# A gated-linear-attention stage written in a new order, on one core of a Trainium2 chip

## What is computed

```python
q, k, v, r, glr = jnp.split(proj, ODD_SPLITS, axis=-1)
gate_logit = glr @ w_gate2.astype(jnp.float32) + b_gate.astype(jnp.float32)
log_a = (jax.nn.log_sigmoid(gate_logit) / GLA_TAU).reshape(B, T, GLA_HEADS, GLA_DK)
# per chunk, with b the running sum of log_a in the chunk
w = jnp.exp(jnp.where(causal[None, :, :, None, None], diff, -jnp.inf))
scores = jnp.einsum('bihd,bjhd,bijhd->bhij', qc, kc, w)
o = (jnp.einsum('bhij,bjhe->bihe', scores, vc)
     + jnp.einsum('bihd,bhde->bihe', qc * jnp.exp(b), s))
s = (s * jnp.exp(b_last)[..., None]
     + jnp.einsum('bjhd,bjhe->bhde', kc * jnp.exp(b_last[:, None] - b), vc))
# then
o = head_rms(o) * norm_w.astype(jnp.float32)
mix = (jax.nn.silu(r) * o.reshape(B, T, GLA_VALUE)).astype(h.dtype) @ w_out
```

## Time and profile before

| | |
|---|---|
| median of 3 runs | 2778.07 us (2776.79 to 2779.69) |
| profiled execution, its own time | 2778.14 us |
| its span | 2776.3 us |
| PE busy | 2638.2 us (95%) |
| DVE, ACT, POOL busy | 1361.3, 643.9, 853.0 us |
| mean granted clock of PE | 0.959 |

### The profile page before, as it was taken

The page is one execution under the profiler, slowest core; times in us unless marked ns, Lnnn a source line. Parts: engine busy times, 40 slices in busy tenths (PEclk is TensorE's granted clock), DMA queues, the critical chain, the costliest instruction groups (busy, mean ns, idle before and its releaser), DMA issues.

```text
span 2776.3 us, 38625 instructions
## 1 busy us (share of the span) xinstructions
PE 2638.2 (95%) x15232; PEld 2516.0 (91%) x15232; DVE 1361.3 (49%) x2146; ACT 643.9 (23%) x1111; POOL 853.0 (31%) x383
## 2 busy tenths in 40 slices
PE   7999879999999999999989999897999999999998
PEld 7898639999999999999878888787999999999997
DVE  6763355553344344436565656554553443343345
ACT  3610142321011011113223434432230110011013
POOL 3332103333333333333211112112433333333340
PEclk9999959999999999999989989888999999999999
DMA  3011002111111111112101010102111111111111
GB/s 133 31 56 39 31 25 103 46 46 46 47 39 46 47 46 46 39 45 110 39 18 54 25 54 25 54 18 110 43 42 46 46 46 39 47 46 46 46 54 65
DMA packets 39152, 137.63 MB, mean 50 GB/s; under 512 B 5952, under 2 KB 9664, under 8 KB 37712
## 3 DMA queue, kind: packets, MB, share of 16 engines
q1 hardware_dynamic: 32192, 104.55, 11.4%
q10 hardware_dynamic: 6800, 30.71, 2.9%
HBM read 120.36 MB, written 14.88 MB: 49 GB/s over the span
## 4 chain that ended last, share of the span: by engine, by line
issue 54%; PE 30%; POOL 14%; DVE 1%; DMA 1%; POOLq 1%; ACT 0%; SPq 0%; ACTq 0%; DVEq 0%
PE PS L498 30%; POOL WH L468 8%; POOL WL L471 6%; DMA WR<-ws 0%; DVE RA L1250 0%; DVE X L1299 0%; DMA X<-xT 0%; POOLq L467 0%; POOLq L479 0%; DVE X L1260 0%; POOLq L470 0%; PE PS L623 0%; SPq L441 0%; DVE X L1311 0%; PE PS L549 0%
## 5 line engine op out<-in xcount | busy, mean ns | idle before, releaser
L498 PE MATMUL PS<-RA,WH 128*128 128x384 f32 (+1 forms) x4608 | 1134.3, 330 | 36.0 <-issue 13.0
L498 PE MATMUL PS<-RB,WH 128*128 128x384 f32 (+1 forms) x4272 | 1060.0, 332 | 4.1 <-DVE X L1260 4.1
L468 POOL TENSOR_TENSOR WH<-WR,ZERO 128x1024 fp32r<-128x1024 f32 x185 | 355.4, 1921 | 1843.0 <-PE PS L498 1833.9
L498 PEld LDWEIGHTS PS<-RA,WH 128*128 128x128 f32 x4608 | 818.3, 189 | 47.8 <-issue 31.4
L498 PEld LDWEIGHTS PS<-RB,WH 128*128 128x128 f32 x4272 | 761.3, 190 | 19.6 <-issue 11.9
L498 PE MATMUL PS<-RA,WL 128*128 128x384 f32 (+1 forms) x2304 | 755.8, 328 | 0.0
L498 PE MATMUL PS<-RB,WL 128*128 128x384 f32 (+1 forms) x2136 | 701.4, 328 | 0.0
L471 POOL TENSOR_TENSOR WL<-WR,WH 128x1024 fp32r<-128x1024 f32 x185 | 480.3, 2596 | 14.5
L498 PEld LDWEIGHTS PS<-RA,WL 128*128 128x128 f32 x2304 | 435.3, 189 | 0.0
L1260 DVE TENSOR_TENSOR X<-PS,X 128x384 f32<-128x384 f32 x360 | 189.7, 534 | 440.7 <-PE PS L498 440.7
L498 PEld LDWEIGHTS PS<-RB,WL 128*128 128x128 f32 x2136 | 405.2, 190 | 0.0
(11 more groups left out here) (195 smaller groups left out, 1739.1 us busy)
## 6 DMA issues: line engine op xcount, KB each, us to landing
WR<-ws SPq DMA_DIRECT2D x189, 512.0 KB, 3.3
X<-xT ACTq DMA_DIRECT2D x8, 544.0 KB, 7.8
EB<-xT ACTq DMA_DIRECT2D x8, 544.0 KB, 8.1
x_spill<-X ACTq DMA_DIRECT2D x1, 4352.0 KB, 12.1
EB<-x_spill ACTq DMA_DIRECT2D x8, 544.0 KB, 7.1
GA<-st_gla ACTq DMA_DIRECT2D x4, 1024.0 KB, 5.3
glas_o<-GA ACTq DMA_DIRECT2D x4, 1024.0 KB, 3.9
yT<-X SPq DMA_DIRECT2D x16, 192.0 KB, 1.9
```

What stands on the lines that cost most here:

```text
L468: nc.gpsimd.tensor_tensor(WH[:, slot, :], WR[:, slot, :], ZERO[:, 0:1].to_broadcast([P, 1024]), ALU.add).then_inc(w_high, 1)
L498: return nc.tensor.matmul(out, lhsT, rhs, start=start, stop=stop, skip_group_check=True)
```

## The change

The stage's list is written anew, and with it the emitted parts:

- **All gate logits first.** The weight tile of "low" holds its 16 columns three times (at 0, 32, 64), and so does the gate weight. Item GL rounds both stacks on ACT and makes the remainder of one copy of each on DVE (L1620), so that one matmul over 96 partitions (L770) gives the three products of the split. The 12 logit matmuls (L, banks 6 and 7 in turn) stand in the projections of k0 and v0; softplus and sums (SPA, SPD) are done per head over all 1088 tokens, into tiles of X.
- **Chunks pipelined.** C1 and C2 become A and B. At place k of 36 the list has A of chunk k+1, S, B of chunk k, S; transposed keys and values and scores have two tiles each (gKVT, gSC). The state products move from A to B. Preparation of the next group (KD, DE, X, XE, Q, P) stands in the first two of each three places; the levels are scored from 6 down to 0, and level 0 takes the keys as they are, which saves a difference, an exponential and a product.
- **Samples third from last.** Chunk 8 stands between chunks 5 and 6; its eight updates are four pairs (CB), with one masked-key product for all eight (L1739).
- **GNM** has one matmul, since DVE adds the two squares first (L1769).
- **Roundings ahead.** MIX rounds and splits six of the eight tiles of the output projection's input before the list ends, and two after it.

The diff's core:

```diff
+ORDER = [0, 1, 2, 3, 4, 5, 8, 6, 7]
+    x = lambda v: [("X", e, v), ("XE", e, v)]
+    q = lambda v: [("Q", e, v)]
+    return [[[("KD", e), ("DE", e)] + x(6) + x(5), x(4) + q(6), x(3) + q(5) + x(2)],
+            [q(4) + x(1) + [("XE", e, 0)], [("P", e)] + q(3) + q(2), q(1) + q(0)]]
...
+    s = low + q0 + [("GL",), ("L", 0, 0)] + k0[:1] + [("L", 0, 1), ("SPA", 0, 0, 1)] + k0[1:2] + [("L", 0, 2)] + k0[2:]
+    s += [("SPD", 0, 0, 1), ("SPA", 0, 1, 3)] + L(1) + v0[:1] + [("SPD", 0, 1, 3)] + L(2) + v0[1:2] + L(3)
+    first, then = prepare(0)
+    s += [("SPA", h, 0, 3) for h in range(1, GH)]
+    s += first[0] + first[1] + v0[2:] + first[2] + v1[:1] + then[0] + then[1] + v1[1:2] + then[2]
+    s += [("SPD", 1, 0, 3)] + v1[2:] + [("A", 0, 0), ("SPD", 2, 0, 3), ("SPD", 3, 0, 3)]
     for h in range(GH):
...
+            if k + 1 < len(PLACES):
+                s.append(("A",) + PLACES[k + 1])
+            if p % 3 == 0 and e:
                 s.append(("GNM",) + divmod(e - 1, 3))
+            s += prep[0] + mine[:1]
+            if last:
+                s += [("MIX", 0), ("MIX", 1)]
+            s.append(("B", h, c))
+            if p % 3 == 0 and e:
+                s.append(("GN2",) + divmod(e - 1, 3))
+            if c == LAST:
+                s += [("CB", h, 0)] + mine[1:] + [("CB", h, 1)] + prep[1] + [("CB", h, 2), ("CB", h, 3)] + prep[2]
             else:
+                s += prep[1]
+                if last:
+                    s += [("MIX", 2), ("MIX", 3)]
+                s += mine[1:] + prep[2]
+            if p % 3 == 2:
+                s.append(("GN1", h, p // 3))
+    s += [("MIX", 4), ("GNM", GH - 1, 2), ("MIX", 5), ("GN2", GH - 1, 2), ("GMIX",), ("MIX", 6), ("MIX", 7)]
...
+                    pe.wait_ge(gl_ready, 2)
+                    if i < 2:
+                        pe.wait_ge(rs_log, 3 * 3)
+                    else:
+                        pe.wait_ge(lg_read, i - 1)
+                    nc.tensor.matmul(PS[:, 6 + i % 2, 0:size], WGH[:, GDK * h:GDK * (h + 1)], GLH[:, s:s + size],
                                      start=True, stop=True).then_inc(lg_done, 1)
...
+                elif kind == "GL":
+                    dve.wait_ge(gl_high, 2)
+                    for out, of in ((WGH[64:96, :], WG2[64:96, :]), (GLH[32:64, :], GLR[32:64, :])):
+                        V.tensor_tensor(out, of, out.bitcast(F32), ALU.subtract).then_inc(gl_ready, 1)
...
+                elif kind == "MIX":
+                    k = item[1]
+                    if k == 3:
+
+                        dve.wait_ge(gsb_stored, 16 * GH)
+                    if k == 6:
+                        dve.wait_ge(go_done, len(PLACES))
+                        dve.wait_ge(gp_stored, 16 * GH)
+                    low(4, k, RA1, None)
```

More of the change, by code:

```diff
@@ L803, in _ @@
                                   c == 0 and v == 0, v == 1)
                     last.then_inc(go_done, 1)
[L805 to L812 removed]
+                    if ahead("GNM", *item):
+                        pe.wait_ge(gn_log, ahead("GNM", *item))
```

523 lines of the change are left out of this document (274 added, 249 removed).

## The result

The changed kernel takes 2745.86 us (median of 4 runs, 2744.86 to 2751.67), where the kernel before, with a fourth run beside it, takes 2777.43. The ratio is 0.9894, 95% interval 0.9879 to 0.9909: faster by 1.06%, 31.6 us of medians. Forecast were 71 us and 2707. The sign holds, and the size does not: less than half came. 2745.86 lies inside the whole range (2655 to 2752), which was widened to take in two rivals, and outside the forecast's own (2685 to 2730).

What follows compares the result with a forecast made beforehand. Prediction: PE is bound by 70 us of idle and 62 lost to a slow clock in the GLA stage. Front -12, head 0 +5, heads 1 and 2 +43, head 3 +27, end +8 make 71: 2778 to 2707; range 2655 to 2752.

Steps and rivals of the forecast that it cites:

- the clock term: Whole stage: of 62 us lost to PE's slow clock, 46 come back and 15.5 are left.
- The second hangs on the first: GLA stage: the 62 us lost to the clock follow from PE's 70 us of idle gaps.
- its link to the gaps is what failed: Stated disproof: clock under 0.93 in heads 1 and 2 although PE waits little.
- The front: Projections ahead of the first chunk: four new logit waits, 10.1 us, plus 2 of clock; a loss of 12.
- Heads 1 and 2: Waits on L747 and the update go; idle 5, clock 2, work 3.3 a head; 43 us gained together.
- Without that cover each would return at its own length: Heads 1 and 2: masks and ACT's copy, if not covered, would each cost 2 to 3 us.
- Head 0: Late level products, masks and preparation: idle 22 against 15.1, clock 6 against 15.1, work 3.3; 5 us gained.
- Head 3 and the end: Head 3 gains 27 us; the gap and first output step gain 8, with the seventh tile 7 late.
- The work: PE loses one large product per GNM and has cheaper logits: 3.3 us a head saved, none by sample pairs.
- The pipeline holds from the start: Rival, 20 in 100: ACT and DVE get through the front in PE's shadow; 114 us gained, 2664.
- DVE paces everywhere: Rival, 14 in 100: weight splits hold DVE up, preparations 3 to 4 us late; 37 gained, 2741.
- The slower case: Rival, 4 in 100: 11 preparations late, from 5 us each eating the gain; at 8 us each, 2820.

Runs made afterwards that it cites:

- e1_spread: Changed kernel with S groups put between the sample pairs (two places in heads 1 to 3, one in head 0): 2728.59 us, ratio 0.9828.
- e4_together: Changed kernel with the sample place's second S group moved ahead of the pairs, so all four pairs follow one another: 2743.01 us, ratio 0.9872.
- e10_unpiped: Changed kernel with A of the next chunk behind both S groups, except each head's last chunk; a store on ACT moves too: 2751.34 us, ratio 0.9909.
- e5_mix_end: Changed kernel with all eight roundings and remainders (MIX 0 to 7) at the end of the list again: 2752.52 us, ratio 0.9905.

## Why the prediction was wrong

**The step that failed** is the clock term, in two places. The first is "The second hangs on the first", that is, clock loss follows gaps. From it came a clock of 0.98 in heads 1 and 2 (2 us lost each) where 0.92 was granted (9.8 each), and the whole clock term of 46 us, where 6 came. Gaps do bring half clock, but a run of narrow products does so as well with PE busy, and the change put three pairs end to end in every head where heads 1 and 2 had had one or two samples among S groups. These gap-less stretches are 22 us of the 55.9 lost. e1_spread and e4_together show it from both sides, and the earlier trace rows had the hint: head 3, whose samples stand without S groups, had the lowest clock of the heads. The second is the price of the gaps that were left. Before, 12.2 us of idle in head 1 cost 13.0 of clock; for heads 1 and 2 the prediction set 2 beside an idle of 5 and gave no reason, and for head 0 it took little "since a slow PE where DVE paces only shortens the next wait". Measured were 34 us behind gaps in the whole stage where 15.5 was all that was to be left; in heads 1 and 2 some 5 each behind 6.8 of idle. So of the 40 us that the clock term lacks, 22 are stretches with no gap ahead, behind narrow products, and 18 are stretches behind gaps, priced too low. The last thing the prediction named as what could prove it wrong ("its link to the gaps is what failed") is what happened, and it is half of what failed.

**The front** had the right mechanism and terms too small: GL 5.9 for 3.5, the sixth logit 6.0 for 2.2, L(2,2) 3.9 for 3.6, L(3,1) 1.0 for 0.8, and 6.9 of clock loss for 2. The first two are those on which a weight split fell. I priced one beside POOL and not the other, although both stand at the end of a weight step, where POOL always starts.

**Heads 1 and 2** otherwise: the waits on L747 and on the update went, as said. GNM's waits were taken as 0.4 each and came to 2.9 a head, nearly all of it in one, where the addition stands at the end of a chain on ACT and DVE; the pairs' 1.5 stood as a wait of 1.4 on the masked keys, not on the last pairs. Idle was 6.8 for 5. "Without that cover each would return at its own length" was too much for the chunks: e10_unpiped took most of the cover away, its masks waited 14.7 us for 5.8, and its time is the changed kernel's within 8 us.

**Head 0** came within 3 by two errors that cancel: idle 17.4 for 22, because the third chunk waited 0.4 for its masks and not 3.6 and the second preparation was 1.9 late and not 4, and clock 13.5 for 6. The terms ahead of chunk 0's scores and chunk 1's masks were right in kind and size (2.9 for 4, 5.4 for 6.4).

**Head 3 and the end.** "The last GNM, whose addition stands on DVE behind four remainders" was named, and was given no price of its own; it was 8.6 us, and the output projection began 9.6 late. The seventh tile's 7 us, which I put inside the first output step, were not seen (13.3 for 13.9). The end gave 4.2, not 8. By e5_mix_end the roundings' whole worth is less than two sets of runs tell.

**The work** was right: 13.2 forecast, about 15 measured. The pairs may be some of the rest: four take 8.0 us at full clock (1.94 and 2.10 each above), eight singles some 9.6 (1.06 and 1.33 from one's start to the next in head 1). I had said that nothing was saved there.

**The rivals.** "The pipeline holds from the start" did not come, as the front's waits were orders. (Its sum counts head 3's gain twice; it should be 111, 2667.) "DVE paces everywhere" gave 2741, near the measured time, but by a mechanism that the trace denies: the three preparations of heads 1 and 2 cost PE 1.0 us a head on level products, not 9. POOL's splits do fall on them (P's product L1688 takes 2.75 beside one and 0.55 alone), but what they hit most is the norm. The slower case and the one without effect did not occur.

**What the change is worth** is then this: its work (15 us), and the logits taken out of bank 7, of whose 20.3 us the front kept 16.8. The pipelined scores and the roundings ahead each change nothing that these runs can tell, which is to within 8 us; for the scores the two As end to end hide what the edit alone would do. The state products' move into B was not tried alone. Three gaps of 1.2 us, which the profile puts down to issue, stand ahead of the next head's first A (1479.59 in head 0). That A turns a value tile whose first group was projected just before it, and it waits for DVE to have read that group (`psum_free`): DVE's reading (L1270) runs from 1478.94 to 1479.49. This is a reading of kernel and trace; no run tried it, but in e10_unpiped, where two more S groups stand ahead of that A, the gaps are gone.

## What to carry to other kernels

When the clock of a stretch is low, list every slow interval with what PE did ahead of it, not only the sum: slow intervals without a gap ahead are a cause of their own, here small products placed end to end, and here the cure was to put them among wide ones. Price the gaps that will be left by what such gaps cost before. In a kernel in which all engines follow one list, an item moved out of a wait stands in front of something else; ask for each move what now comes due at that moment, and whether another engine's burst (a weight split) starts at the same event. Undo parts alone before crediting them: here two of the most laborious parts gave nothing that could be measured.
